# Two transformer blocks on one core: the second block's recurrence and sparse attention put in another order

## The reference, cut to what matters

```python
qkv_a = silu(causal_depthwise_conv(qkv_a, conv_w))          # 3 x 4 heads x 128
q_a = l2_normalize(q_a) * 128 ** -0.5;  k_a = l2_normalize(k_a)
beta = sigmoid(beta_a);  g = -exp(a_log) * softplus(alpha_a + dt_bias)
# gated delta rule, chunks of 64: gc = cumsum(g) in the chunk, decay[i,j] = exp(gc_i - gc_j), i >= j
a_low = strict((k * beta) @ k.T * decay);  ia = I + a_low
u = solve(ia, v * beta);  w = solve(ia, k * beta * exp(gc))
qk = (q @ k.T) * decay;  qg = q * exp(gc);  kd = k * exp(gc_last - gc)
for each chunk: v_new = u - w @ S;  o = qg @ S + qk @ v_new;  S = S * exp(gc_last) + kd.T @ v_new
o_a = rmsnorm(o) * gain * silu(z)                            # per head
# native sparse attention: 8 heads; rotary q and keys; 15 compressed keys; a selected and a window branch
o_b = g0 * attn(q, k_cmp) + g1 * attn(q, k_slc) + g2 * attn(q, k_win)
merged = sigmoid(merge_a) * (o_a @ w_gdn) + sigmoid(merge_b) * (o_b @ w_nsa)
x = x + merged @ w_out;  x = x + (silu(h2 @ w_gate) * (h2 @ w_up)) @ w_down;  out = rmsnorm(x)
```

## Time and profile before

| | value |
|---|---|
| runs | 988.01, 990.68, 991.35 us |
| profiled execution | 989.6 us, its span 987.8 us |
| PE busy | 927.0 us (94%) |
| DVE, ACT, POOL busy | 564.3, 427.4, 57.4 us |
| granted PE clock, mean | 0.97 |
| the second block's projections begin | about 471 us |
| level(1) begins | 601.6 us |
| first merge product begins | 735.9 us |

### The profile page before, as it was taken

How to read it: one execution, slowest core, us unless ns; L and a number is a source line. 1 busy time by engine, 2 the same in 40 slices (tenths; PEclk the granted TensorE clock), 3 DMA queues, 4 the chain that set the end, 5 groups by cost and what they waited for, 6 DMA issues and landing times.

```text
span 987.8 us, 13268 instructions
## 1 busy us (share of the span) xinstructions
PE 927.0 (94%) x5520; PEld 807.5 (82%) x5520; DVE 564.3 (57%) x805; ACT 427.4 (43%) x568; POOL 57.4 (6%) x72
## 2 busy tenths in 40 slices
PE   6999999999999999997999897999689999999996
PEld 6989998899997888875999786887457788888885
DVE  4845565646566655554695736345456565565543
ACT  6643446543445444443654202434343344444331
POOL 1000000000200000002000304100000000000000
PEclk9999999999999999999899978999879999999999
DMA  9558543454454445664577321342014545655541
GB/s 306 173 200 241 177 162 112 153 193 148 157 176 162 158 162 170 201 232 159 180 171 185 115 84 47 127 108 64 1 43 168 181 140 171 193 190 172 173 166 43
DMA packets 127490, 152.30 MB, mean 154 GB/s; under 512 B 16919, under 2 KB 93078, under 8 KB 127302
## 3 DMA queue, kind: packets, MB, share of 16 engines
q1 hardware_dynamic: 127290, 151.36, 48.1%
q0 software_dynamic: 64, 0.07, 0.0%
q10 hardware_dynamic: 76, 0.02, 0.0%
HBM read 149.32 MB, written 3.68 MB: 155 GB/s over the span
## 4 chain that ended last, share of the span: by engine, by line
PE 87%; DVE 6%; ACT 2%; issue 2%; POOL 1%; DMA 1%; ACTq 0%; POOLq 0%; DVEq 0%
PE bank L494 24%; PE bank L495 24%; PE bank L496 24%; PE bank L890 1%; DVE arena L1935 1%; PE bank L950 1%; PE bank L559 1%; PE bank L965 1%; PE bank L883 1%; PE bank L960 1%; PE bank L640 1%; PE bank L620 1%; DVE w_lo L1719 1%; PE bank L996 1%; ACT w_hi L1286 1%
## 5 line engine op out<-in xcount | busy, mean ns | idle before, releaser
L1719 DVE TENSOR_TENSOR w_lo<-ring,w_hi 128x2048 fp32r<-128x2048 f32 (+2 forms) x133 | 299.6, 2255 | 230.2 <-ACT w_hi L1286 230.0
L1286 ACT ACTIVATE w_hi<-ring 128x2048 fp32r<-128x2048 f32 (+2 forms) x133 | 250.0, 1881 | 142.8 <-PE bank L496 131.9
L494 PE MATMUL bank<-h_hi,w_hi 128*128 128x256 f32 (+1 forms) x640 | 185.0, 289 | 1.4 <-DVE h_lo L1756 1.4
L495 PE MATMUL bank<-h_lo,w_hi 128*128 128x256 f32 (+1 forms) x640 | 182.9, 286 | 0.0
L496 PE MATMUL bank<-h_hi,w_lo 128*128 128x256 f32 (+1 forms) x640 | 182.8, 286 | 0.0
L494 PE MATMUL bank<-w_hi,h_hi 128*128 128x512 f32 (+1 forms) x400 | 155.1, 388 | 0.7 <-DVE h_lo L1756 0.7
L496 PE MATMUL bank<-w_hi,h_lo 128*128 128x512 f32 (+1 forms) x400 | 152.7, 382 | 0.0
L495 PE MATMUL bank<-w_lo,h_hi 128*128 128x512 f32 (+1 forms) x400 | 152.4, 381 | 0.0
L494 PEld LDWEIGHTS bank<-h_hi,w_hi 128*128 128x128 f32 (+1 forms) x640 | 123.8, 194 | 3.4 <-issue 3.1
L495 PEld LDWEIGHTS bank<-h_lo,w_hi 128*128 128x128 f32 (+1 forms) x640 | 123.9, 194 | 0.4 <-issue 0.2
L496 PEld LDWEIGHTS bank<-h_hi,w_lo 128*128 128x128 f32 (+1 forms) x640 | 123.8, 194 | 0.0
(11 more groups left out here) (317 smaller groups left out, 1299.1 us busy)
## 6 DMA issues: line engine op xcount, KB each, us to landing
ring<-in_w_in SPq DMA_DIRECT2D x60, 1024.0 KB, 4.9
ring<-in_w_gate_up SPq DMA_DIRECT2D x44, 512.0 KB, 4.4
ring<-in_w_down SPq DMA_DIRECT2D x10, 1024.0 KB, 5.0
ring<-in_w_mem_kv SPq DMA_DIRECT2D x8, 1024.0 KB, 7.0
ring<-in_w_gla_out SPq DMA_DIRECT2D x4, 1024.0 KB, 4.9
ring<-in_w_x_out SPq DMA_DIRECT2D x4, 1024.0 KB, 4.9
ring<-in_w_dsa_out SPq DMA_DIRECT2D x4, 1024.0 KB, 5.9
ring<-in_w_o SPq DMA_DIRECT2D x4, 1024.0 KB, 5.0
```

What stands on the lines that cost most here:

```text
L494: mm(o, ah, bh, start=start, stop=False, skip_group_check=True)
L495: mm(o, ah, bl, start=False, stop=False, skip_group_check=True)
L1286: act(w_hi[:, k % NHI, 0:m], ring[:, order.index(name) % NSLOT, 0:m], ACT.Copy)\
L1719: tt_(w_lo[:, i, 0:m], ring[:, i, 0:m], w_hi[:, k % NHI, 0:m].bitcast(F), ALU.subtract)\
```

## The change

Four things are done in the second block, and nothing outside it.

1. **Norms.** `nr` and `rb` go away, with the DVE passes that scaled q and k. The key norm enters as a number per row where keys are already multiplied by one: in the columns of `kbe` (4:8), of `vb` (16:20) and of `nA` (20:24), so that the solve works on scaled unknowns. The query norm joins the normalization of the output (`sumsq` is taken with the norm as scale, `r8` multiplies it in).
2. **Preparation.** `gb`, `kg`, `ss`, `qg`, `kk`, `vt` and the rotary products stand between the projections `c3` to `z1`; `vsvw` is projected last. On DVE, ACT and POOL the work that belongs to them moves with them.
3. **Levels.** The head steps of sparse attention take the place of the wide projections between `level` and `level_end`; the compressed branch's two softmax steps (`compressed_max`, `compressed_norm`) stand there too.
4. **Recurrence.** `ma0`, `ma1`, `mb0`, `mb1` come after it has begun: `gdn_chunk(1)`, (2), (3) between their halves, `gdn_state` between them, `gd` ahead of `mb1`. The merge computes `bn0`, `bn1` ahead of `gt`, `bg0`, `bg1`.

```diff
@@ PE, preparation
-            for j in range(3, 6):
-                project_channels(f"c{j}", h_parts)
-            project_channels("kcks", h_parts)
...
-            pe.wait_ge(signal("norm_cols"), 1)
-            bank = open_bank("nr")
...
-                    ins = mm(bank[:, 256 * hh:256 * hh + 256], rowsel[0:8, 2 * j + hh, :], norm_rows, start=True, stop=True)
-                done(f"rb{j}", ins)
+            project_channels("c3", h_parts)
+            for j in range(2):
+                bank = open_bank(f"gb{j}")
...
+            project_channels("c4", h_parts)
+            project_channels("c5", h_parts)
+            project_channels("kcks", h_parts)
+            project_channels("kwvc", h_parts)
...
+            pe.wait_ge(signal("silu_done"), 4)
+            head_products("kg", 4)
+            project_channels("nq0", h_parts)
+            pe.wait_ge(signal("squares"), 4)
+            bank = open_bank("ss")
...
+            head_products("qg", 0)
+            pe.wait_ge(*read("kwvc"))
+            rope_turn("r0", 0, 2)
+            rope_turn("r1", 2, 1)
+            project_channels("nq1", h_parts)
+            head_transposes("kk", 4)
+            pe.wait_ge(*read("nq0"))
+            rope_turn("r2", 4, 2)
+            project_channels("z0", h_parts)
+            pe.wait_ge(signal("silu_done"), 6)
+            head_transposes("vt", 8)
+            pe.wait_ge(*read("nq1"))
+            rope_turn("r3", 6, 2)
+            project_channels("z1", h_parts)
...
+            project_tokens("vsvw", h_parts)
@@ PE, levels, heads, recurrence
-            level(1)
-            wide_tokens("ma0", h_parts)
-            level_end(1)
...
+            level(1)
+            compressed_keys()
+            nsa_logits(0)
+            nsa_logits(1)
+            level_end(1)
+            compressed_scores()
+            nsa_step(0)
+            level(2)
+            nsa_step(1)
+            nsa_step(2)
+            level_end(2)
+            compressed_transposes()
+            nsa_step(3)
+            level(3)
+            nsa_step(4)
+            nsa_step(5)
+            level_end(3)
+            nsa_step(6)
+            nsa_step(7)
+            level(4)
...
+            gdn_state(0)
+            wide_tokens("ma0", h_parts, lambda: gdn_chunk(1))
+            gdn_state(1)
+            wide_tokens("ma1", h_parts, lambda: gdn_chunk(2))
+            gdn_state(2)
+            wide_tokens("mb0", h_parts, lambda: gdn_chunk(3))
+            gdn_out()
+            wide_tokens("mb1", h_parts)
...
+            merge_part("bn", 0, (oT_hi, oT_lo))
+            merge_part("bn", 1, (oT_hi, oT_lo))
...
+            merge_part("bg", 0, (z2_hi, z2_lo))
+            merge_part("bg", 1, (z2_hi, z2_lo))
@@ POOL
-            gp.wait_ge(*read("rb1"))
+            gp.wait_ge(signal("egc"), 2)
             gp.wait_ge(signal("decay2"), 1)
+            gp.wait_ge(signal("silu_done"), 2)
             nc.gpsimd.tensor_tensor(egc, egc, cv[:, 0:4, :], ALU.mult).then_inc(signal("q_decayed"), 1)
@@ DVE
+                if j == 4:
+                    decays()
...
+            ve.wait_ge(signal("norm_cols"), 1)
+            step(tt_(cols[:, :, 24:28], cols[:, :, 0:4], a_cols[:, :, 4:8], ALU.mult))
+            step(stt(cols[:, :, 20:24], cols[:, :, 24:28], -1.0, a_cols[:, :, 4:8], ALU.mult, ALU.mult))
+            tsc(cols[:, :, 16:20], cols[:, :, 24:28], 0.5, None, ALU.mult)
+            step(stt(cols[:, :, 4:8], cols[:, :, 20:24], -1.0, cols[:, :, 4:8], ALU.mult, ALU.mult))
...
+            level_add(3)
+            for i in range(6, 10):
+                nsa_step(i)
+            level_add(4)
```

More of the change, by code:

```diff
@@ L1057, in gdn_state, with compressed_keys @@
                 done(f"gs{c}", ins)
+            def compressed_keys():
+                pe.wait_ge(*read("hid"))
+                pe.wait_ge(signal("w2_in"), 32)
+                bank = open_bank("kcv")
+                for g in range(2):
+                    mm(bank[64 * g:64 * g + 64, 0:15], w2k, hid[:, 15 * g:15 * g + 15], start=True, stop=True)
+                for g in range(2):
+                    ins = mm(bank[0:15, 64 + 64 * g:128 + 64 * g], hid[:, 32 + 15 * g:47 + 15 * g], w2v, start=True, stop=True)
+                done("kcv", ins)
@@ new lines, in _ @@
+            nsa_step(11)
+            level(5)
+            nsa_step(12)
+            nsa_step(13)
+            level_end(5)
+            nsa_step(14)
+            for t in range(TT):
+                pe.wait_ge(*read(f"xt5{t}"))
+                bank = open_bank(f"u{t}")
+                for h in range(4):
+                    ins = mm(bank[:, 128 * h:128 * h + 128], TmT[:, 4 * t + h, :], vb[:, 4 * t + h, :], start=True, stop=True)
+                done(f"u{t}", ins)
+                bank = open_bank(f"wt{t}")
+                for h in range(4):
+                    ins = mm(bank[:, 128 * h:128 * h + 128], kbe[:, 4 * t + h, :], TmT[:, 4 * t + h, :], start=True, stop=True)
+                done(f"wt{t}", ins)
@@ L1520, in _ @@
             conv_tanh(5)
+            square_of(2)
+            square_of(3)
             copy("kwvc", pair(ns, 1))
-            copy_tokens("vsvw", v_tok)
+            sc.wait_ge(signal("d_min"), 1)
+            act(nA, nA, ACT.Exp, scale=-1.0).then_inc(signal("d_exp"), 1)
+            act(qkT, qkT, ACT.Exp).then_inc(signal("d_exp"), 1)
             copy("nq0", pair(ns, 2))
             copy("nq1", pair(ns, 3))
-            sc.wait_ge(signal("silu_done"), 6)
-            for j in range(4):
-                act(pair(sq, j), pair(cv, j), ACT.Square, scale=0.5).then_inc(signal("squares"), 1)
@@ L2241, in _ @@
+            for c in range(2):
+                for t in range(TT):
+                    title = f"bn{c}{t}"
+                    v = mb[:, t, 512 * c:512 * c + 512]
+                    bank_ready(title)
+                    stt(v, v, 1.0, bank_of(title)[:, :], ALU.add, ALU.mult).then_inc(reader(title), 1)
             for j in range(2):
```

630 lines of the change are left out of this document (307 added, 323 removed).

## The result

The changed kernel takes 952.03 us (median of 4 runs, 951.25 to 952.84) against 989.35 us for the kernel before, timed beside it: ratio 0.963, 95% interval 0.961 to 0.965. The profiled execution took 951.25 us, 38.4 less than the one of before.

What follows compares the result with a forecast made beforehand. Bound by PE: 216.1 us of second-block work plus charges of 1 (preparation), 17 (levels), 1 (recurrence) and 4 (merge) gave 239.1 against 266.6, 27.5 less; 989.6 became 962.1, stated as 962.5, range 948 to 979.

Steps and rivals of the forecast that it cites:

- all of it hides: Rival, whole second block: waits of 8 us in the levels, 2.8 in the merge, none elsewhere; 949.9 us, chance 0.12.
- signs: Second block: level(1) near 576 us, clock 1.0, no earlier wait above 2; levels 73 to 76; gapless projections; 3 us merge gap.
- Norms: Second block: nr and rb leave PE with 4.5 and 0.6 us of waits; POOL's power, about 3.4 us, costs nothing.
- Preparation: Up to level(1): 80.9 us of PE work plus 1 us of waiting for kwvc's low part, bounds 0 and 6.
- Levels: Heads in the levels: 57.9 us of PE work plus 17 of waits and half clock, bounds 8 and 32.5.
- The last copies: End of the levels: copies ahead of the fourth product with v make PE wait 1.5 us.
- Half clock: Levels with heads: small work leaves PE less than full, charged 3 us of half clock.
- Recurrence: Recurrence beside the wide projections: 54.2 us of PE work plus 1 us of waits, bounds 0 and 3.
- Merge: Merge products and gt: 22.6 and 0.9 us, plus 4 for the kept 2.8 us gap and 1.2 of half clock.
- Bound by the chain: Rival, levels: chain-bound as the heads were, 32.5 us instead of 17; 977.6 us, chance 0.20.
- POOL blocks DVE: Rival, preparation: POOL's passes hold two-input DVE passes, PE waits 6 us for w_lo; 968.5 us, chance 0.08.
- Half clock through the levels: Rival, levels: 75 us without a projection may keep PE at 1.2 GHz; up to 1017.4 us, chance 0.05.

Runs made afterwards that it cites:

- the wrong mask: Changed kernel with norm ahead of level additions, gt between bn0 and bn1, q product later, plus POOL's level 3 mask behind level 1's last transposes: 937.75 us, ratio 0.949.
- the preparation alone: Only the change's norms and preparation; levels, heads, recurrence and merge ordered as in the kernel before: 966.13 us, ratio 0.977 against the kernel before.

## Why the prediction was right, and where a term was off

The time lies in the range, yet 10.5 us under the forecast of 962.5 and nearest to the rival "all of it hides" (949.9). Three of the four stretches came within 0.3 us; the forecast missed by the fourth. Of its signs all came but one: from `level(1)` to the last product with v it was to take 73 to 76 us and took 64.7. `level(1)` began at 574.9 us (576 forecast), with no wait above 0.88 us ahead of it and a clock of 1.00.

*Norms.* As forecast. POOL's power takes 2.93 us and PE waits for it nowhere.

*Preparation.* 82.2 us against 81.9. The 1 us was charged for `kwvc`'s low half, and PE waited 0.88 there and nowhere else. The reason was half right: DVE is short by its own work (three clips more lengthen the wait by their whole 2.15 us), but the last microsecond came from POOL, since the wait goes with the q product.

*Levels.* This is the term that was mis-sized, by 10.2 us of the sum. Three parts:
- Waits of PE: 14 charged, 6.0 measured. At levels 3 to 5, 2.5 each were charged for additions and norm; the trace shows 1.91, 1.91 and 0. The chain was named correctly, and moving the norm ahead of the additions takes it away. But the additions of the last bank and the norm run while PE still transposes one head, and its half microsecond was named in the text and not subtracted; at level 5 the products `u` and `wt`, 3.6 us by the same text, lie ahead of head 15 and cover it. Levels 1 and 2 cost 2.2 instead of 5, and 1.5 of this is POOL's mask. The last copies cost nothing.
- Work: with the waits and the half clock away the stretch takes 56.57 us, of which 1.7 are waits: 54.9, not 57.9. The product with v was priced at 2.6 us from a partial row; the timeline of PE in the changed kernel has 597.73 to 599.75, 2.0 us, and there are four:

```profile
597.73 1.52 PE L957 MATMUL bank<-arena 128*64 128x256 f32 x16
599.18 0.65 PE L961 MATMUL bank<-arena 15*64 15x256 f32 x4
599.75 2.05 PE L911 MATMUL bank<-arena 128*128 128x128 f32 x16
```

- Half clock: 3 charged, two spells of 3.4 us, at half rate 1.7 each, so 3.4.

*Recurrence.* 55.0 against 55.2, with no wait. That the projections cover waits and keep the clock up there is shown by the recurrence without them: 10.7 us more.

*Merge.* 27.8 against 27.5: a gap of 2.62 where 2.8 was kept, a spell of 3.4 us (1.7 lost) where 1.2 was added.

*The rivals.* "All of it hides" was close in the levels (waits and half clock of 9.4 where it had 8, and less work); elsewhere it lacked the 0.9 us of the preparation and the 1.7 of half clock in the merge. "Bound by the chain" needed 32.5 us of waits and half clock. "POOL blocks DVE" is real as a mechanism and small in size: about 1 us of it reached PE in the preparation, and 1.5 in the levels. POOL was busy 23.5 us in the preparation, 20.6 without its power, where 14.7 were counted: a third level mask fell into it, and two masks took 6.8 us there that take 2.36 each elsewhere. The Trainium skill, "SBUF — State Buffer", section "Who interferes with whom", says that the engine that issues first holds the shared ports for its whole instruction and that a `tensor_scalar` can need them too, not only an operation with two inputs. The traces agree: 0.70 against 1.75 us for the clip, 0.16 against 2.25 for the product of 128x2. "Half clock through the levels" is refuted by the window of 41 us at 1.00.

## What to carry to other kernels

A wait between two small groups of matmuls can cost more than its length, and what removed it here was the order of two short operations on the engine that feeds PE: put the one that PE needs next ahead of the one that it needs a level later. Fill a chain that hands back and forth between engines with work that needs nobody, here a wide projection; done bare, the same chain cost 10.7 us. When two edits differ by less than single executions do, read the changed part from the trace beside the time, and keep an edit that should do nothing, like the wrong mask here, to tell the two apart. When you charge a wait, subtract the work that PE has in hand, and look for what comes between in its list.

## What the runs showed of the hardware

- A DVE operation can lose nearly the whole of a POOL pass however small it is: a product of 128x2 lost 2.1 us to a mask of 2.36 us, a clip of 128x1024 1.05 us to a product of 2.41 us that had begun 1.2 us earlier. Where in the order a long POOL pass starts matters more than how much of it there is: 23.5 us of POOL in the preparation cost PE 0.9 us, one mask of 2.36 us in the levels 1.5.
- Short waits of PE bring half clock, the longer the surer. In the changed part, over the profiles of the changed kernel and its variants other than the preparation alone, a spell of 3.4 us at 0.50 began at the wait's end or up to 1.3 us after it behind 1 of 10 waits of 1.53 us, 6 of 12 of 1.91, 6 of 6 of 2.62 and the one of 3.07; behind single waits of 0.9 and 1.2 us none did. The preparation alone has a wait of 2.78 without one. In the bare recurrence six waits of about 1 us went with 17 us at 0.50. What decides in the single case wasn't tried. Without such waits, small matmuls back to back held the full clock for 41 us.
